# A tile-wise first step with early transposes in feed-forwards 2 to 4, and an attention that begins with the first tile's values

## The reference

```python
def swiglu(x, w_in, w_out):
    gu = x @ w_in
    g, u = gu[..., :D_FF], gu[..., D_FF:]
    return (jax.nn.silu(g) * u) @ w_out

for l in range(DEPTH_2):                      # 2 layers
    x = layer_norm_2(ALPHA_2 * x + 0.5 * swiglu(x, ffn_w_in[l, 0], ffn_w_out[l, 0]), ln_g[l, 0], ln_b[l, 0])
    y = mlstm_mixer(...) if l % N_MIXERS == 0 else window_attention(...)
    x = layer_norm_2(ALPHA_2 * x + y, ln_g[l, 1], ln_b[l, 1])
    x = layer_norm_2(ALPHA_2 * x + 0.5 * swiglu(x, ffn_w_in[l, 1], ffn_w_out[l, 1]), ln_g[l, 2], ln_b[l, 2])
```

## Time and profile before

| | us |
|---|---|
| median of 3 runs | 1694.98 (1694.79 to 1697.49) |
| profiled execution, its own time | 1697.26 |
| its span | 1695.5 |
| TensorE busy | 1592.3 (94%) |
| VectorE busy | 779.7 (46%) |
| ScalarE busy | 505.8 (30%) |
| mean granted TensorE clock | 0.976 |

### The profile page before, as it was taken

One profiled execution on the slowest core, in us unless ns is written; L12 is line 12 of the kernel. 1 busy time (PEld: TensorE's weight loads), 2 busy tenths in 40 slices (PEclk: granted clock), 3 DMA queues, 4 the chain that ended last, 5 costly groups with the idle time before them and its releaser, 6 DMA issues.

```text
span 1695.5 us, 21971 instructions
## 1 busy us (share of the span) xinstructions
PE 1592.3 (94%) x9238; PEld 1172.1 (69%) x9238; DVE 779.7 (46%) x1028; ACT 505.8 (30%) x573; POOL 61.4 (4%) x104
## 2 busy tenths in 40 slices
PE   8997899999999998999998899999999997899997
PEld 7744433333333336999896689998999986689997
DVE  1584411111111116544656675456544566564445
ACT  1251100000000003334354234342443435433432
POOL 2000000000000000000000000000000000000000
PEclk9997899999999999999999999999999998999999
DMA  6705799999999999753223578554554221387500
GB/s 198 250 1 232 290 415 429 428 429 429 428 428 429 429 412 353 268 183 114 75 78 122 174 243 292 185 185 161 202 190 157 98 76 74 100 288 264 193 0 26
DMA packets 149457, 395.27 MB, mean 233 GB/s; under 512 B 9442, under 2 KB 109920, under 8 KB 136592
## 3 DMA queue, kind: packets, MB, share of 16 engines
q1 hardware_dynamic: 146656, 385.67, 60.5%
q0 software_dynamic: 2736, 8.68, 1.4%
HBM read 393.28 MB, written 1.05 MB: 233 GB/s over the span
## 4 chain that ended last, share of the span: by engine, by line
PE 67%; DMA 14%; DVE 10%; issue 3%; SPq 3%; ACT 2%; POOL 1%; POOLq 0%; DVEq 0%; ACTq 0%
PE bank L1355 29%; DMA ring<-in_moe_w_dram 14%; PE bank L1368 12%; PE bank L885 8%; PE bank L914 2%; PE bank L697 2%; SPq L267 2%; PE bank L1343 2%; PE bank L1575 1%; PE bank L902 1%; PE bank L644 1%; PE bank L1900 1%; PE bank L934 1%; DVE stats L539 1%; PE bank L683 1%
## 5 line engine op out<-in xcount | busy, mean ns | idle before, releaser
L885 PE MATMUL bank<-ring,arena 128*64 128x512 f32 x928 | 228.4, 596 | 9.5 <-DMA ring<-in_moe_w_dram 9.5
L1355 PE MATMUL bank<-x_hi,split_u_hi 128*128 128x256 f32 x688 | 194.9, 283 | 0.0
L1355 PE MATMUL bank<-x_hi,split_u_lo 128*128 128x256 f32 x688 | 194.7, 283 | 0.0
L1355 PE MATMUL bank<-x_lo,split_u_hi 128*128 128x256 f32 x688 | 194.7, 283 | 0.0
L1355 PE MATMUL bank<-x_lo,split_g_hi 128*128 128x256 f32 x656 | 185.6, 283 | 0.0
L1355 PE MATMUL bank<-x_hi,split_g_lo 128*128 128x256 f32 x656 | 185.6, 283 | 0.0
L1355 PE MATMUL bank<-x_hi,split_g_hi 128*128 128x256 f32 x656 | 185.6, 283 | 0.0
L885 PEld LDWEIGHTS bank<-ring,arena 128*64 128x64 f32 x928 | 69.3, 137 | 146.3 <-issue 114.7
L1265 DVE TENSOR_TENSOR split_g_lo<-ring,split_g_hi 128x2048 fp32r<-128x2048 f32 x47 | 107.7, 2292 | 127.7 <-ACT split_g_hi L1259 127.7
L1115 DVE SCALAR_TENSOR_TENSOR arena<-arena,work 128x256 f32<-128x256 f32 x32 | 15.5, 485 | 287.7 <-PE bank L934 287.7
L1265 DVE TENSOR_TENSOR split_u_lo<-ring,split_u_hi 128x2048 fp32r<-128x2048 f32 x45 | 103.1, 2292 | 69.0 <-ACT split_u_hi L1259 69.0
(11 more groups left out here) (352 smaller groups left out, 2504.8 us busy)
## 6 DMA issues: line engine op xcount, KB each, us to landing
ring<-in_moe_w_dram SPq DMA_DIRECT2D x92, 2048.0 KB, 19.1
ring<-in_ffn_w_in_dram SPq DMA_DIRECT2D x88, 1024.0 KB, 5.5
ring<-in_ffn_w_out_dram SPq DMA_DIRECT2D x44, 1024.0 KB, 5.5
ring<-in_ml_w_in_dram SPq DMA_DIRECT2D x12, 1024.0 KB, 5.2
ring<-in_rec_w_in_dram SPq DMA_DIRECT2D x10, 1024.0 KB, 11.6
ring<-in_at_w_in_dram SPq DMA_DIRECT2D x6, 1024.0 KB, 5.2
ring<-in_rec_w_out_dram SPq DMA_DIRECT2D x5, 1024.0 KB, 13.6
gb_row<-in_ln_g_dram POOLq DMA_DIRECT2D x8, 512.0 KB, 7.3
```

The costliest lines, as they stand in the source:

```text
L885: i = nc.tensor.matmul(bank[4 + p][64 * j:64 * j + 64, :], xe[p][:, k, :], unit_view(n, 4)[:, k % 4, :], start=(k == 0), stop=(k == KT - 1))
L1355: i = nc.tensor.matmul(up_bank(kind, s_)[:, m * T:(m + 1) * T], w, xp_[b][:, k, :], start=(k == 0 and j == 0), stop=(k == KT - 1 and j == 2))
```

## The change

It has these parts.

- **Early transposes.** For norms 3 to 6 the transposes of tile 0 stand ahead of group (1,1) of the stage before, and those of tile 1 behind the work on tile 0. No warming matmuls run at these norms.
- **Tile-wise first step.** In feed-forwards 2 to 4 step 0 has x stationary, one token tile at a time, and the weights of g and u moving: 48 matmuls for tile 0, transposes of tile 1, 48 matmuls for tile 1. h then has tokens on partitions; four transposes between the up projections of step 1 turn it into bank 4.
- **Weights of step 0** of these feed-forwards lie split in the ring (two slots for each unit) instead of in the split buffers. g and u of step 0 are both split before the norm: behind the mixers for feed-forwards 2 and 4, and in step 9 of feed-forward 2 for feed-forward 3. The splits of step 1 come first in the feed-forward.
- **x_lo of tile 0** is made within the norm, ahead of the last residual.
- **Attention.** Values of tile 0 (24 matmuls), transposes of tile 1, keys (48), values of tile 1 (24); the banks are renamed to suit.
- Two semaphores of the first block are merged into one.

```diff
+                if f > 0 and kind < 2 and s_ == 0:
+                    units.append((k, src, (f_mm[kind], NSTEP * f + 1)))
+                    units.append((0, None, (f_mm[kind], NSTEP * f + 1)))
+                else:
+                    units.append((k, src, (f_lo[kind], NSTEP * f + s_ + 1)))
...
+            def low_part(t, b):
+                dve.wait_ge(G["ln_evac"], 4 * L + 2 * t + b + 1)
+                nc.vector.tensor_tensor(x_lo[:, 4 * b:4 * b + 4, t * P:(t + 1) * P], turned(t, b),
+                                        x_hi[:, 4 * b:4 * b + 4, t * P:(t + 1) * P].bitcast(F32), ALU.subtract) \
+                    .then_inc(G["ln_lo"], 1)
...
+            if L in TILE_NORMS:
+                low_part(0, 0)
+                low_part(0, 1)
...
+                for t, b in ((1, 0), (1, 1)) if L in TILE_NORMS else ((0, 0), (1, 0), (0, 1), (1, 1)):
+                    low_part(t, b)
...
-        def norm_pe(pe, L):
-            for t in range(TT):
-                keep_warm(pe, WARM[t])
+        def norm_pe(pe, L, tiles=range(TT), warm=None):
+            for t in [tiles] if isinstance(tiles, int) else tiles:
+                keep_warm(pe, WARM[t] if warm is None else warm)
...
+            if f > 0 and kind < 2 and s_ == 0:
+                n = at_unit["f", f, kind, 0]
+                return ring_r[:, (n + 1) % RING, :], ring_r[:, n % RING, :]
+            return [part[:] for part in slots(f)[0 if kind == 2 and s_ == NSTEP - 1 else kind]]
...
+            elif f > 0 and (kind, s_) == (0, 1):
+                act.wait_ge(f_mm[1], NSTEP * f)
+            elif f > 0 and (kind, s_) == (1, 1):
+                act.wait_ge(G["ln_in"], 4 * (NORM_AFTER[f - 1] + 1))
...
+                by_tile = f > 0 and s_ == 0
                 act.wait_ge(f_mm[0], c + 1)
                 if c:
                     act.wait_ge(f_h, c)
                 nc.scalar.activation(silu, up_bank(0, s_)[:].rearrange("p (a t) -> p a t", a=2),
                                      ACT.Silu).then_inc(f_silu, 1)
-                split_act(act, f, *((0, s_ + 1) if s_ < NSTEP - 1 else (2, s_)))
-                act.wait_ge(f_h, c + 1)
-                nc.scalar.activation(h_hi[:, s_ % 2], h_raw, ACT.Copy).then_inc(f_hhi, 1)
-                if s_ < NSTEP - 1:
-                    split_act(act, f, 1, s_ + 1)
-                    split_act(act, f, 2, s_)
+                if not by_tile:
+                    split_act(act, f, *((0, s_ + 1) if s_ < NSTEP - 1 else (2, s_)))
+                if by_tile:
+                    act.wait_ge(f_turn, f)
+                    nc.scalar.activation(h_hi[:, 0], h_turned, ACT.Copy).then_inc(f_hhi, 1)
+                    split_act(act, f, 2, 0)
+                else:
+                    act.wait_ge(f_h, c + 1)
+                    nc.scalar.activation(h_hi[:, s_ % 2], h_raw, ACT.Copy).then_inc(f_hhi, 1)
+                    if s_ < NSTEP - 1:
+                        split_act(act, f, 1, s_ + 1)
+                        split_act(act, f, 2, s_)
+                if f == 1 and s_ == NSTEP - 2:
+                    split_act(act, 2, 0, 0)
+                    split_act(act, 2, 1, 0)
...
-            split_dve(dve, f, 1, 0)
+            if f == 0:
+                split_dve(dve, f, 1, 0)
+            else:
+                split_dve(dve, f, 0, 1)
+                split_dve(dve, f, 1, 1)
...
+        def norm_and_ffn_pe(pe, f, L):
+            n_split = SPLIT_NORMS.index(L)
+
+            def first_of_tile(t, part):
+                x = xp_[part]
+                for k in range(KT):
+                    if k % 4 == 0:
+                        if part == 0:
+                            pe.wait_ge(G["ln_evac"], 4 * L + 2 * t + k // 4 + 1)
+                        else:
+                            pe.wait_ge(G["ln_lo"], 4 * n_split + 2 * t + k // 4 + 1)
+                    for kind in range(2):
+                        for n, w in enumerate(place_of(f, kind, 0)[0:2 - part]):
+                            i = nc.tensor.matmul(bank[kind][:, t * FSTEP:(t + 1) * FSTEP], x[:, k, t * P:(t + 1) * P],
+                                                 w[:, k * FSTEP:(k + 1) * FSTEP],
+                                                 start=(t == 0 and part == 0 and k == 0 and n == 0),
+                                                 stop=(part == 1 and k == KT - 1), skip_group_check=True)
+                        if part == 1 and t == 1 and k == KT - 1:
+                            i.then_inc(f_mm[kind], 1)
+
+            pe.wait_ge(f_lo[0], NSTEP * f + 1)
+            pe.wait_ge(f_lo[1], NSTEP * f + 1)
+            first_of_tile(0, 0)
+            first_of_tile(0, 1)
+            norm_pe(pe, L, 1, 0)
+            first_of_tile(1, 0)
+            first_of_tile(1, 1)
+            ffn_pe(pe, f, L)
...
+                        if t == 1 and hf == 1 and NORM_AFTER[f] in TILE_NORMS:
+                            norm_pe(pe, NORM_AFTER[f], 0, 0)
...
-            up_first()
-            up(1, 0, base)
+            if f == 0:
+                up_first()
+                up(1, 0, base)
             for s_ in (1, 2):
                 up(0, s_, base + s_)
+                if f > 0 and s_ == 1:
+                    pe.wait_ge(f_h, base + 1)
+                    for m in range(2):
+                        for t in range(TT):
+                            i = nc.tensor.transpose(h_turned[:, m, t * P:(t + 1) * P], h_raw[:, t, m * P:(m + 1) * P], ident[:])
+                    i.then_inc(f_turn, 1)
...
             project(1, 0, (6, 7))
+            norm_pe(pe, 3, 0, 0)
             project(1, 1, range(KT))
...
+            def values(t):
+                for j, (x, part) in enumerate(((x_hi, 0), (x_hi, 1), (x_lo, 0))):
+                    for k in range(KT):
+                        if t == 0 and k % 4 == 0 and j != 1:
+                            pe.wait_ge(G["ln_lo"] if j else G["ln_evac"], 4 * (n_split if j else 5) + k // 4 + 1)
+                        i = nc.tensor.matmul(bank[0][:, t * T:(t + 1) * T], x[:, k, t * P:(t + 1) * P],
+                                             at_weight(k // 4, 4)[part][:, k % 4, 256:512],
+                                             start=(k == 0 and j == 0), stop=(k == KT - 1 and j == 2))
+                return i
...
+            values(0)
+            norm_pe(pe, 5, 1, 0)
             for low in range(2):
                 for g in range(2):
...
-            i.then_inc(at["v"], 1)
+            values(1).then_inc(at["v"], 1)
...
             project(1, 0, (KT - 1,))
+            norm_pe(pe, 6, 0, 0)
             project(1, 1, range(KT))
...
-            norm_pe(pe, 3)
-            ffn_pe(pe, 1, 3)
-            norm_pe(pe, 4)
-            ffn_pe(pe, 2, 4)
-            norm_pe(pe, 5)
+            norm_and_ffn_pe(pe, 1, 3)
+            norm_and_ffn_pe(pe, 2, 4)
             at_pe(pe)
-            norm_pe(pe, 6)
-            ffn_pe(pe, 3, 6)
+            norm_and_ffn_pe(pe, 3, 6)
...
             ffn_first_act(act, 1)
+            split_act(act, 1, 1, 0)
             norm_evac_act(act, 3)
             ffn_act(act, 1)
-            ffn_first_act(act, 2)
...
             ffn_first_dve(dve, 1)
+            split_dve(dve, 1, 1, 0)
             norm_dve(dve, own, 3, ALPHA_2)
             ffn_dve(dve, 1)
-            ffn_first_dve(dve, 2)
```

More of the change, by code:

```diff
@@ L72 @@
 NORM_AFTER = (2, 4, 5, 7)
+TILE_NORMS = (3, 4, 5, 6)
 class Own:
@@ L574, in norm_dve @@
             if L in SPLIT_NORMS:
-                n = SPLIT_NORMS.index(L)
-                for t, b in ((0, 0), (1, 0), (0, 1), (1, 1)):
-                    dve.wait_ge(G["ln_evac"], 4 * L + 2 * t + b + 1)
-                    nc.vector.tensor_tensor(x_lo[:, 4 * b:4 * b + 4, t * P:(t + 1) * P], turned(t, b),
-                                            x_hi[:, 4 * b:4 * b + 4, t * P:(t + 1) * P].bitcast(F32), ALU.subtract) \
-                        .then_inc(G["ln_lo"], 1)
+                for t, b in ((1, 0), (1, 1)) if L in TILE_NORMS else ((0, 0), (1, 0), (0, 1), (1, 1)):
+                    low_part(t, b)
         def turned(t, b):
@@ L1257, in split_act @@
             here(act, n)
+            if f > 0 and kind < 2 and s_ == 0:
+                here(act, n + 1)
             slot_free(act, f, kind, s_)
-            nc.scalar.activation(place_of(f, kind, s_)[0][:], unit(n), ACT.Copy).then_inc(f_hi[kind], 1)
+            nc.scalar.activation(place_of(f, kind, s_)[0], unit(n), ACT.Copy).then_inc(f_hi[kind], 1)
         def split_dve(dve, f, kind, s_):
@@ L1294, in ffn_dve @@
         def ffn_dve(dve, f):
-            split_dve(dve, f, 1, 0)
+            if f == 0:
[3 more added lines that the diff above has]
+                split_dve(dve, f, 1, 1)
             for s_ in range(NSTEP):
                 c = NSTEP * f + s_
-                split_dve(dve, f, *((0, s_ + 1) if s_ < NSTEP - 1 else (2, s_)))
+                by_tile = f > 0 and s_ == 0
+                if not by_tile:
+                    split_dve(dve, f, *((0, s_ + 1) if s_ < NSTEP - 1 else (2, s_)))
```

(38 more changed lines are left out.)

44 lines of the change are left out of this document (24 added, 20 removed).

## The result

The changed kernel takes 1698.62 us (median of 20 runs, 1696.07 to 1700.92), the kernel before 1695.6 us (20 runs on the same chip, 1693.14 to 1698.28): +3.0 us, ratio 1.0019, 95% interval 1.0012 to 1.0025. The measured ratio lies within 0.2%, which the prediction took as no change, but its interval lies above 1: if anything the kernel is slower. The profiled execution took 1699.29 us, its span 1697.6 us, its mean clock 0.972.

A forecast was written before the change was run, and what follows sets the result against it. TensorE, busy 94% of the span, was taken as the bound, so only its waits could pay. Norms -1.3 us plus low clock +3.4 gave +2.1 on the median 1694.98, about 1697.0 us, range 1692.5 to 1701.0.

The forecast's parts named there:

- The stalls: Ahead of group (1,1), norms 3 to 6: tile 0's transposes wait for scaling, delaying it 5.8, 2.7, 2.6 and 6.4 us.
- The gain of the tile-wise step: First feed-forward step: 48 matmuls per tile in 5.80 us, tile 0's covering tile 1's norm; norm 4 nets -2.2 us.
- The second split: VectorE ahead of norms 3 and 6: splitting u too, 2.29 us, makes the first residual 1.7 and 1.0 us late.
- The clock: Group (1,1) at norms 3 and 6: low clock after each stall costs 1.7 us, +3.4 us in all.
- forecast -1.3: Norms 3 to 6 without clock loss: +1.4, -2.2, -0.7 and +0.2 us, sum -1.3 us.
- the forecast's +0.2: Norm 6 without clock loss: first step ends at 1511.1 instead of 1510.9, +0.2 us.
- Rival C: Low clock at norms 4 and 5 too, or of double length at norms 3 and 6: 1700.5 us, chance 0.19.
- A: The forecast itself: two low-clock stretches, at norms 3 and 6, 1697.0 us, own range 1694.5 to 1699.5, chance 0.49.
- Rival D: Norms 3 to 6: tile 0's transposes cost no stall and no clock is lost, 1680.2 us, chance 0.05.
- rival E: Norms 3 and 6: weights of step 1 load late, g split 4.7 us behind need, 1706.4 us, chance 0.07.

The follow-up runs named there:

- Experiment 1: The changed kernel with tile 0's transposes put back behind group (1,1) at norms 3 to 6, all else as changed: 1683.76 us, ratio 0.9936 to the kernel before.
- Experiment 3: The changed kernel with VectorE's split of u moved behind tile 0's norm at norms 3 and 6: 1695.36 us.
- Experiment 2: The changed kernel with 16 and 18 warming matmuls ahead of tile 0's transposes at norms 3 and 6: 1695.31 us.
- Experiment 4: The kernel before with only tile 0's transposes moved ahead of group (1,1) at norms 3 to 6: 1716.51 us, ratio 1.0126.
- 9: Experiment 4 with 8 unread transposes of the identity added behind group (1,1) at norms 3 to 6: 1714.91 us, ratio 1.0114 to the kernel before.
- 10: Experiment 4 with 8 more warming matmuls behind group (1,1) at norms 3 to 6: 1710.64 us, ratio 1.009 to the kernel before.
- number 5: Experiment 1 with x_lo of tile 0 made later, between tile 1's first centring and its scaling: 1683.5 us, ratio 0.9927 to the kernel before.

## Why the prediction was right

- **The stalls.** Forecast 5.8, 2.7, 2.6 and 6.4 us; from the end of group (1,0) (981.43 + 0.23 = 981.66 at norm 3) to the start of group (1,1) in the chain (988.05) they measured 6.4, 2.8, 2.8 and 7.1. The surplus at norms 3 and 6 is 0.65 us of transposes at low clock each. The idle time ahead of them was forecast as 4.6 and 5.2 us at norms 3 and 6 and 1.6 at norms 4 and 5; it was 4.26, 4.94 and 1.33. Experiment 1 shows that the place of these transposes is what makes VectorE's lag a cost.
- **The gain of the tile-wise step.** Forecast as 48 matmuls in 5.80 us for a tile; they took 5.75 for tile 0 and 6.01 for tile 1, and nothing but the copy was waited for. Norms 4 and 5 came out at -2.2 and -0.6.
- **The second split** made the residual late as forecast: the two splits, 976.36 + 4.49, end as it starts (980.77, the rows overlap by 0.08). Experiment 3 prices it.
- **The clock** was forecast of the right kind and at the right two places, but too small. In the pause of each of norms 3 and 6 a low stretch of double length began, 3.4 us of lost work each by the windows and not 1.7. Part of it fell where TensorE stood still. What reached the path was 0.65 + 1.54 = 2.2 us at norm 3 and 0.65 + 1.90 = 2.55 at norm 6, together 4.75 and not 3.4. Experiment 2 gives the same, 4.7 at these places. Without the clock the four norms come to 3.2 - 4.75 = -1.5 us, forecast -1.3. The low stretch that the kernel before had behind norm 6 (6.82 instead of 5.74 us for its first 48 matmuls) is gone, but that offsets nothing: the forecast's +0.2 had it in its time before (1505.13) already.
- **The number.** Forecast 1697.0, measured 1698.62. Of the 1.6 us, 0.6 is the kernel before (1695.6 over 20 runs, not 1694.98 over 3), and 0.9 the change (+3.0, not +2.1). The clock is the only term that was off by more than 0.2 us at the four norms.
- **Rival C** had two forms, each at 1700.5 us. The second, a low stretch of double length at norm 3 and at norm 6, is what the profile shows. So the account that came true is A's in its places and C's in the length, and the time stayed in A's range because 2.1 of the 6.8 us of lost work fell outside the path. The first form, low clock at norms 4 and 5 too, is not in the changed kernel's profile, where the groups took 2.76 us at both and the keys 5.74. But at norm 5 it is near: the keys took 6.73 us in experiment 1, and in 2 and 3, where the pause ahead of them has the same shape as in the changed kernel, their first 32 took 5.58 and 5.56 instead of 4.06. Experiment 4 had the low clock at all four norms. Whether the other 19 executions of the changed kernel escaped it too isn't shown.
- **Transposes and the clock.** In experiments 9 and 10 the low clock came behind 3 of 4 norms with 8 transposes more, and behind none with 8 warming matmuls more. The Trainium skill says in "TensorE: Matmul & The Clock Gate", Part 4 (PE-mode transpose), that a transpose doesn't count as busy in the way that a matmul does. By that rule 9 would have stayed at the 1716.5 us of 4, and had it counted in full, 9 would have come to 10's 1710.6; it measured 1714.9, nearer to the rule. The two don't weigh equal amounts, though: the transposes add 1.0 us of work, the warming matmuls 1.8, and they leave a pause of 1.2 us ahead of tile 1's transposes against 0.3. So it isn't shown that transposes count for nothing at all, nor that it is their kind and not the shorter work that let the clock fall.
- **Rival D** (no stall) fell by the earlier trace rows and by the wait of 4.26 us; **rival E** (weights of step 1 late) by VectorE's timeline: g was split at 1004.18 + 2.29 = 1006.47, and PE began with it at 1007.76, 1.3 us later; the forecast had 0.8 us to spare.

Open is why one sequence of pause and work is followed by the low clock in one place and not in another: 8 transposes, 8 warming matmuls, 8 transposes in 6.2 us led to it at one of four norms in the profile of the kernel before, and at three of four in experiment 9. The length of the pause doesn't decide it alone: idle for 3.94 us before 963.79 and for 4.64 before 1466.05 in the kernel before, TensorE met a single low stretch, after 4.26 and 4.94 us in the changed kernel a double one.

The best version is number 5 (1683.5 us), with 1 equal to it within the spread: 0.7% below the kernel before and 0.9% below the changed one.
